# mLSTM gate rows and attention norm sums: placed between strips instead of in one piece

## What is computed

```python
def mlstm_prepare(qkv, gate_pre, gate_b):
    q, k, v = jnp.split(qkv.astype(jnp.float32), 3, axis=-1)
    ...
    pre = (gate_pre + gate_b).reshape(b, n, 4, MLSTM_HEADS).transpose(2, 0, 3, 1)
    return to_heads(q), to_heads(k) * MLSTM_HEAD_DIM ** -0.5, to_heads(v), pre

def token_mixers(hx, hc, cos, sin, want_ctx, w_in, ...):
    cu_x, mqkv_x, mo_x, mg_x, aq_x, ak_x, av_x, bg_x = jnp.split(hx @ w_in, offsets, axis=-1)
    cu_c, mqkv_c, mo_c, mg_c, aq_c, ak_c, av_c, bg_c = jnp.split(hc @ w_in, offsets, axis=-1)
    conv_x = conformer_conv(cu_x, conv_dw_w, ...)          # depthwise convolution, 31 taps
    h_x, h_c = mlstm_bidirectional(*mlstm_prepare(mqkv_x, mg_x, mlstm_gate_b), ...)
    k_x = apply_rope(attn_heads(ak_x, ATTN_KV_HEADS, k_norm_w), cos, sin)   # attn_heads: per-head rmsnorm
    q_x = apply_rope(attn_heads(aq_x, ATTN_HEADS, q_norm_w), cos, sin)
    attn_x = latent_attention(q_x, ...) @ w_attn_out
    ...
```

## Time and profile before

| what | value |
|---|---|
| median of 3 runs | 2216.56 us (2213.89 to 2219.6) |
| span of the profiled execution | 2212.6 us |
| TensorE busy | 2160.0 us, 98% |
| VectorE busy | 1675.8 us, 76% |
| ScalarE busy | 963.5 us, 44% |
| GpSimd busy | 109.6 us, 5% |

### The profile page before, as it was taken

How to read it: one execution, slowest core, us unless ns; L and a number is a source line. 1 busy time by engine, 2 the same in 40 slices (tenths; PEclk the granted TensorE clock), 3 DMA queues, 4 the chain that set the end, 5 groups by cost and what they waited for, 6 DMA issues and landing times.

```text
span 2212.6 us, 33802 instructions
## 1 busy us (share of the span) xinstructions
PE 2160.0 (98%) x14082; PEld 1871.5 (85%) x14082; DVE 1675.8 (76%) x3056; ACT 963.5 (44%) x1562; POOL 109.6 (5%) x86
## 2 busy tenths in 40 slices
PE   5999999999999999999999999999999999999999
PEld 4988889978878877778888888867989889998999
DVE  5988879888568686547874899976368767677994
ACT  3557535574433354353222433321344446644552
POOL 0000000000000122210000000000000222100000
PEclk9999999999999999999999999999999999999999
DMA  9874377535231111125552355535542212564553
GB/s 342 281 228 142 126 245 258 162 127 168 82 96 58 58 58 39 39 71 185 182 191 96 123 197 196 197 119 185 163 116 77 77 58 77 181 216 156 191 181 124
DMA packets 280809, 324.53 MB, mean 147 GB/s; under 512 B 28496, under 2 KB 261456, under 8 KB 280528
## 3 DMA queue, kind: packets, MB, share of 16 engines
q1 hardware_dynamic: 280656, 322.36, 45.2%
HBM read 321.29 MB, written 1.05 MB: 146 GB/s over the span
## 4 chain that ended last, share of the span: by engine, by line
PE 84%; DVE 10%; ACT 3%; DMA 1%; issue 1%; POOL 0%; SPq 0%; ACTq 0%; DVEq 0%
PE ps L779 82%; DVE parts L2168 2%; DVE ring L2121 1%; ACT w_high L1576 1%; DMA ring<-w_ada_t 1%; PE ps L1305 1%; DVE arena L2607 1%; DVE arena L2268 1%; DVE parts L2575 1%; ACT hT L1768 0%; POOL parts L2067 0%; DMA c_rows<-c_row 0%; DVE arena L2304 0%; DVE arena L2310 0%; DVE parts L2393 0%
## 5 line engine op out<-in xcount | busy, mean ns | idle before, releaser
L779 PE MATMUL ps<-parts,w_high 128*128 128x256 f32 (+2 forms) x6632 | 1135.2, 321 | 9.1 <-ACT w_high L1576 6.1
L779 PEld LDWEIGHTS ps<-parts,w_high 128*128 128x128 f32 (+1 forms) x6632 | 965.9, 189 | 121.4 <-issue 20.2
L779 PE MATMUL ps<-parts,parts 128*128 128x256 f32 (+1 forms) x3508 | 608.6, 315 | 7.1 <-DVE parts L2393 2.4
L779 PEld LDWEIGHTS ps<-parts,parts 128*128 128x128 f32 x3508 | 508.3, 189 | 57.2 <-DVE parts L2168 3.8
L1576 ACT ACTIVATE w_high<-ring 128x1024 fp32r<-128x1024 f32 (+2 forms) x442 | 439.1, 1011 | 257.2 <-PE ps L779 145.2
L2575 DVE TENSOR_TENSOR parts<-ring,w_high 128x1024 fp32r<-128x1024 f32 (+2 forms) x282 | 323.5, 1153 | 119.5 <-ACT w_high L1576 119.3
L2121 DVE CUSTOM_DVE_ANT_0 ring<-ring,c_rows,cols 128x1024 f32<-128x1024 f32 x144 | 183.0, 1279 | 23.9 <-DMA ring<-ada_w_t 8.9
L2067 POOL TENSOR_TENSOR parts<-ring,w_high 128x512 fp32r<-128x512 f32 x80 | 109.2, 1391 | 1778.6 <-ACT w_high L1576 1778.6
L779 PE MATMUL ps<-arena 128*64 128x256 f32 (+7 forms) x928 | 180.3, 393 | 1.0 <-DVE arena L2772 0.6
L2607 DVE SCALAR_TENSOR_TENSOR arena<-arena,cols 128x512 f32<-128x512 f32 (+1 forms) x240 | 159.5, 664 | 6.2
L779 PEld LDWEIGHTS ps<-arena 128*128 128x128 f32 (+2 forms) x928 | 121.2, 169 | 46.3 <-issue 19.1
(11 more groups left out here) (272 smaller groups left out, 1781.8 us busy)
## 6 DMA issues: line engine op xcount, KB each, us to landing
ring<-w_in SPq DMA_DIRECT2D x118, 1024.0 KB, 5.3
ring<-ada_w_t SPq DMA_DIRECT2D x48, 1024.0 KB, 4.9
ring<-ffn_w_up SPq DMA_DIRECT2D x44, 1024.0 KB, 5.1
ring<-w_ada_t SPq DMA_DIRECT2D x24, 1024.0 KB, 7.2
ring<-w_out SPq DMA_DIRECT2D x16, 1024.0 KB, 5.0
ring<-ffn_w_down SPq DMA_DIRECT2D x16, 1024.0 KB, 5.0
ring<-w_out SPq DMA_DIRECT2D x16, 512.0 KB, 4.7
ring<-w_mlstm_out SPq DMA_DIRECT2D x8, 1024.0 KB, 5.0
```

The costliest lines, as they stand in the source:

```text
L779: return tensor.matmul(o, a, b, start=first, stop=last)
```

## The change

The work stays the same: the same matmuls, evacuations, roots and scans. Three orders change.

- TensorE, keys: the gate rows of kind g stand behind key strip g, for g = 0 to 3, instead of all four behind strip 1.
- TensorE, queries: the 20 (layer 1: 12) sums of squares are cut in three. Those of the keys and of the first query strip stand behind `mq` 0, two more query strips behind `mq` 1, the last behind `mq` 2.
- ScalarE: the evacuation of gate rows g follows `keys(g)`, and so the absolute value, exponential and logarithm follow `keys(3)` instead of `keys(1)`. The roots follow the evacuation of `mq` 2 instead of `mq` 1.

```diff
-                project("mk", 1, 0)
                 for g in range(4):
+                    project_strip("mk", g, 0)
                     u = unit(("mg", l, g))
                     pe.wait_ge(*when(("g_raw", l)))
                     for at in range(0, ROWS, 32):
                         i = mm(u[at:at + 32, :], ident[0:16, g * 4:g * 4 + 32], g_raw)
                     i.then_inc(*pe.step(("full", ("mg", l, g))))
-                project("mk", 4, 0, 1)
+                project("mk", 4, 0, 2)
...
-                def qk_sums():
-
-                    u = unit(("qksum", l))
-                    for t in range(5):
+                def qk_sums(tiles):
+
+                    u = unit(("qksum", l)) if tiles[0] == 0 else ps[:, units[("qksum", l)], :]
+                    for t in tiles:
...
-                    i.then_inc(*pe.step(("full", ("qksum", l))))
+                    if tiles[-1] == 4:
+                        i.then_inc(*pe.step(("full", ("qksum", l))))
...
-                project_slot("mq", 0, lo)
-                qk_sums()
-                project_slot("mq", 1, lo)
+                project_strip("mq", 0, lo)
+                qk_sums((0, 1))
+                project_strip("mq", 1, lo)
+                qk_sums((2, 3))
+                project_strip("mq", 2, lo)
+                qk_sums((4,))
+                project_strip("mq", 3, lo)
                 qk_spread()
...
-                keys(0)
-                keys(1)
                 for g in range(4):
+                    keys(g)
                     a.wait_ge(*when(full(("mg", l, g))))
                     scalar.activation(g_x[:, g, :], bank(("mg", l, g))[0:ROWS, :], ACT.Identity, bias=mgb[:, l, g:g + 1]).then_inc(*a.step(("g_x", l, g), read(("mg", l, g))))
...
-                for t in range(2, KT):
+                for t in range(4, KT):
                     keys(t)
...
-                    if t == 1:
+                    if t == 2:
                         a.wait_ge(*when(full(("qksum", l))))
```

More of the change, by code:

```diff
@@ L1174, in second_layer, with project_strip @@
                 values(1, range(KT))
+                def project_strip(part, t, lo, branch=()):
+                    name = (part, l) + branch + (t // 2,)
+                    take(name)
+                    strip_name = (part, l) + branch + (t,)
+                    u = unit(strip_name)
+                    i = split_strip(u[:, lo:TT], name, t % 2, lo)
+                    i.then_inc(*pe.step(("full", strip_name), ("used", name), ("used_half", half_no[name, t % 2])))
                 def project_slot(part, s, lo, branch=()):
-                    name = (part, l) + branch + (s,)
-                    take(name)
                     for j in range(2):
-                        strip_name = (part, l) + branch + (2 * s + j,)
-                        u = unit(strip_name)
-                        i = split_strip(u[:, lo:TT], name, j, lo)
-                        i.then_inc(*pe.step(("full", strip_name), ("used", name), ("used_half", half_no[name, j])))
+                        project_strip(part, 2 * s + j, lo, branch)
                 def project(part, n, lo, begin=0):
```

## The result

| | median (us) | lowest to highest | span of its profile (us) |
|---|---|---|---|
| before | 2216.56 | 2213.89 to 2219.6 | 2212.6 |
| after | 2231.08 | 2227.93 to 2233.24 | 2227.6 |

The ratio after/before is 1.0052, 95% interval 1.0039 to 1.0066: the changed kernel is slower by 9 to 15 us. The forecast was 2221.7 us with 2215 to 2227 around it, and "the same" as its likeliest case. The time lies outside the range, and by the forecast's own line of 0.3% the kernel is slower, not the same.

The account below looks back on a forecast made before the run. TensorE, busy 2160.0 of 2212.6 us, was taken to bound the kernel, losing by waits or low clock. Layer 0 +1.7 and layer 1 +3.4 us gave +5.1: 2221.7 us, range 2215 to 2227, chance 0.53.

Parts of the forecast that it names:

- The chain of Part 2: Keys: later logarithm delays high and low parts; TensorE passes `mk` 7 3.4 us later in layer 0, 2.8 in layer 1.
- (a): Rival at the new `mk` 7 waits: waits come but the clock holds; +1.8 us, 2218.4 us, chance 0.20.
- (b): Rival at `mk` 7: its low part is in time, no wait; -7.4 us, 2209.2 us, chance 0.05.
- (d): Rival at the sums: 2.0 us pieces still lower the clock; +6.8 us, 2223.4 us, chance 0.05.
- roots, table load and reciprocals fit in there: Queries: roots one strip later are still ready for the spreading behind `mq` 3, 5.4 us after the last sum (layer 1: 2.8).
- VectorE's lateness of 5.1 us: Layer 1: VectorE's delay at the low part of `mk` 7 stays unchanged up to the copy of `mcol`.
- 0.6 us for the scores: Layer 1 scores: VectorE's late `mcol` copy makes them 3.4 us later, where TensorE alone would be 2.8.
- rival (c): At the `mk` 7 waits: clock falls during the wait, each costs 3.4 us; +8.5 us, 2225.1 us, chance 0.17.
- One low stretch, 1.7 us: Behind each new `mk` 7 wait: one low-clock stretch losing 1.7 us, bounds 0 and 3.4 us.
- Part 1, the edges: Gate rows between key strips: 0.09 us at start and 0.15 at end, 1.10 us a kind, 0.7 us more each layer.
- Part 3, the gain at the sums: Queries: sums in three pieces avoid low clock, gaining 3.4 us in layer 0 and 1.7 us in layer 1.
- The 3.96 us that I put between span and median: Whole kernel: median before lay this far above its span; same added to the predicted span 2217.7 us gives 2221.7 us.

Follow-up runs that it names:

- e5: Changed kernel with ScalarE making the high part of `mk` 6 ahead of the evacuation of `mk` 3 and the logarithm: 2217.75 us, ratio 1.0001.
- e3: Kernel before with only the sums' part of the change: sums in three pieces, roots behind `mq` 2, gate rows in one piece: 2219.01 us, ratio 1.0.
- e10: Changed kernel with layer 1's sums in two pieces and its roots behind `mq` 1: 2223.82 us, ratio 1.0023.
- e9: Changed kernel run once more, no edit: 2232.2 us, ratio 1.0046 to the kernel before.
- e11: e7 with the sums and roots as in the kernel before: 2218.11 us, ratio 0.9987.
- e2: Kernel before with only the keys' part of the change, sums and roots as before: 2228.66 us, ratio 1.0042.
- e1: Kernel before run once more, no edit: 2217.26 us, ratio 0.9994.
- e8: Kernel before with the gate rows in one piece behind `mk` 3, evacuations and logarithm behind `keys(3)`: 2226.13 us, ratio 1.0034.
- e4: Changed kernel with VectorE's scans moved behind the low part of `aq` 0: 2224.58 us, ratio 1.0019.
- e7: e6 with gate rows in pairs behind `mk` 0 and `mk` 1 and the high part of `mk` 4 ahead of the evacuations: 2212.92 us, ratio 0.9978.
- e6: e5 with layer 1's sums in two pieces and its roots behind `mq` 1: 2214.79 us, ratio 0.999.

## Why the prediction was wrong, point by point

**The chain of Part 2: right.** Worked out were the low parts of `mk` 6 and 7 at 662.3 and 676.07 and TensorE at 677.3 us; with 4.55 us taken off they stand at 662.6, 676.4 and 677.6 us. Layer 1: TensorE predicted at 1690.0, found at 1690.3 (1698.24 less 7.96). The waits were 4.53 and 3.47 us against 4.8 and 3.7. e5 shows that the chain goes through the high part behind the logarithm. Rivals (a), (b) and (d) fell: the clock did not hold behind the waits, the waits came, and no piece of 2.0 us or less of gate rows or sums was followed by a low stretch in any profile.

**Part 3, "roots, table load and reciprocals fit in there": the step that failed first.** I asked whether the roots are in time for the spreading on TensorE. I did see that VectorE waits longer at its reciprocals, but gave that wait no time in layer 1, and took VectorE's lateness of 5.1 us as a constant carried through to the copy of `mcol`. It was 5.5 us at the low part of `mk` 7 (1696.97 - 7.96 less 1683.55) and 7.2 at the copy (1749.31 - 7.96 less 1734.15). The 1.62 us of waiting at the reciprocals were made up: VectorE's idle time between the two is 1.57 us in before and 1.62 in after. What was not made up is the 1.7 us by which the rows of the rotation, now later, are stretched more than before while GpSimd runs. I had 0.6 us for the scores beyond TensorE's own lateness. To these came 2.0 us (the scores at 1749.67 - 7.96 = 1741.7 instead of 1739.7) and the low stretch behind the wait of 2.52 us, another 1.7: 3.7 us, which is all of layer 1's excess. That the roots' place starts this is shown: e3 has the wait without the keys' part and e10 the keys' part without the wait. That GpSimd stretches the rows is read from the profiles only.

**The clock behind the wait of layer 0: rival (c) was right.** Its condition was that the clock falls while TensorE still waits. It did, with 0.6 us of the wait to come, and the table behind e9 bears the condition out at every wait. One low stretch, 1.7 us, was the term; the stretch in after is 6.82 us long with 6.21 us of work in it, so 3.1 us were lost, and 1.4 of the 1.75 us missing in layer 0 are that. e9 shows that it is no constant of the place: the same 4.52 us were followed by 3.4 us there, the clock having fallen just behind the wait's end. Which of the two comes is chance in one execution. With one or two stretches a wait of this kind costs 1.7 to 3.4 us, and the single value was mis-sized as well as the certainty with which 0.53 was put on it.

**Part 1, the edges: right in kind, short by a tenth.** TensorE's timeline of after around the gate rows of kind 0, and its weight loads, beside the earlier trace rows:

```profile
634.60 1.98 PE L779 MATMUL ps<-parts,parts 128*128 128x512 f32 x8
...
638.31 1.05 PE L779 MATMUL ps<-arena,cst 16*32 16x512 f32 x6
639.30 2.11 PE L779 MATMUL ps<-parts,w_high 128*128 128x512 f32 x8
641.24 1.98 PE L779 MATMUL ps<-parts,parts 128*128 128x512 f32 x8
```

```profile
638.31 0.15 PEld L779 LDWEIGHTS ps<-arena,cst 16*32 16x32 f32 x6 [0.35 <-issue]
639.30 1.68 PEld L779 LDWEIGHTS ps<-parts,w_high 128*128 128x128 f32 x8 [0.84 <-issue]
```

From one strip's second pass to the next are 6.64 us, so a kind costs 6.64 - 5.44 = 1.20 us and not 1.10: the first pass behind it takes 1.94 us instead of 1.81, which I had not priced. That is 0.4 us a layer, and 0.3 of it reach the end of the chain. The loads began with their matmuls on both sides of the gate rows, as the row of before had it. By the rule of the Trainium skill ("TensorE: Matmul & The Clock Gate", Part 2, "Step-by-step: what each phase is for") that a weight load is pulled ahead of running matmuls if the row groups do not conflict or if it goes to the background buffer, the 0.34 us of edges a kind would have been absent; the rows do not show that for these small loads beside wide ones.

**Part 3, the gain at the sums: right in this profile, and less on average.** No low stretch stands behind the pieces, and the 3.4 and 1.7 us came back. But I took them from one profile. Behind sums in one piece the low clock lasted 6.8 us (layer 0) and 3.4 us (layer 1) in before and in e11, 3.4 and 3.4 in e2, 3.4 and none in e1 and e8. In one piece, the gate rows of layer 0 were followed by 3.4 us in before and e1 and 6.8 in e3 and e8, those of layer 1 by 3.4 us in before, 6.8 in e1 and none in e3 and e8. What a cut can win is the mean of these, and the profile of before happened to show much of it at the sums of layer 0.

**The sum.** Predicted +5.1 us; the two layers gave 3.45 + 7.1 = +10.5 us. Of the 5.4 us between, 3.7 are the scores of layer 1 (the 0.3 us by which the chain came later there are in them), 1.4 the second low stretch of layer 0, and 0.3 the chain of layer 0. The last 4.5 us of the profiled difference are the first block's chance. The 3.96 us that I put between span and median were of the same sort: a profiled execution of after had a time of 2229.43 us for a span of 2227.6, 1.8 us more, so the median of before was some 2 us above its profiled execution by chance. I had read 0.3% as "what can be told" and the middle of my sum as well inside it; with the scores of layer 1, the second low stretch and the edges each short on the slow side, the kernel went over it.

## What to carry to other kernels

When a small result is moved later, follow it through every in-order engine's list and not only to the engine that uses it next: here a high part queued behind the logarithm and reciprocals queued ahead of low parts each became a wait of TensorE several strips away, which moving work ahead of the late result cured (e5) and moving its consumer only passed on (e4). A burst that lowers TensorE's clock is worth breaking up only as far as nothing comes later by it, since every wait of 2 to 5 us in the second block cost itself and the low clock behind it: two pieces at the old place (e7) won 0.2%, with the high part made ahead, where four pieces, two strips later, lost 0.5%. Low stretches come and go between executions of one kernel, so look at more than one profile before a gain is credited from them.

## What the runs showed of the hardware

- Low clock followed shorter waits than the 2.43 us in the earlier trace rows too. Waits of 1.98, 2.19 and 2.31 us (e4) and of 2.52 us (after, e3) were followed by 3.4 us at 0.50, the 2.36 us of e5 by 6.8 us; even behind the 0.86 us of e6, with the `mcol` transposes ahead, the clock was 0.50 from 1734.1 us for 3.4 us. The 1.65 us of e8 and the 0.41 us of e10 were not followed by low clock.
- A longer wait is not always followed by it. In the first block TensorE waits for the same high part until 145 to 147 us in every profile: 2.32 us in before and 3.39 us in e3 (to 146.34 us) were followed by full clock, 3.06 us in after by 6.8 us at 0.50, and 3.48 us in e8 by 3.4 us.
- How long it stays low is not fixed by the wait's length: behind 4.53 us it was 6.8 us in after and e2 and 3.4 us in e10; behind 3.47 us it was 3.4 us in after and 6.8 us in e2. It was 6.8 us where the clock fell 0.6 to 1.3 us before the wait's end, and 3.4 us where it fell 0.2 us before it or behind it (the table behind e9).
- Some of VectorE's rotation rows that read two SBUF tiles took much longer beside GpSimd's `TENSOR_TENSOR` (L2074 in after): 1.40 us for one that took 0.42 us alone, 1.65 us for one that took 0.69 us. Rows of the same group that read PSUM kept their 0.69 us. This is seen in the profiles and was not tested.
- The clock also fell with TensorE never idle, behind gate rows or sums in one piece (2.6 to 5.0 us): always in layer 0, and in layer 1 in two of four profiles behind the gate rows and in three of five behind the sums. Behind pieces of 2.0 us or less it fell in none of the profiles (after, e2 to e7, e9 to e11).
- The first 577 us of one and the same kernel took 5.3 us more in one execution than in another, with low stretches at 147.2, 297.4, 491.9 and 498.7 us. Profiled spans of the kernel before were 2212.6 and 2220.3 us; a difference of one profiled pair of under 8 us says nothing by itself here.
